# Two layers of a hybrid attention, Fourier and state-space block: the rotated queries as two products, and three moved pieces of work

## The chip, the cores and the metric

The kernel runs on one core of a Trainium2 chip. The metric is the device time of one execution in microseconds (us). The engines are TensorE (PE; PEld is its weight load), VectorE (DVE), ScalarE (ACT), GpSimd (POOL) and SyncE (SP), which issues DMAs.

## The reference, cut to what matters

Two layers; each has a mixer of three branches (attention with low-rank queries and keys, a Fourier mix, a state-space scan) and an MLP. The change is in the attention. Every head has a query of 64 plain and 32 rotary channels; the rotary key is shared by all eight heads.

```python
def apply_rope(x, cos, sin):
    h = QK_ROPE // 2
    x1, x2 = x[..., :h], x[..., h:]
    return jnp.concatenate([x1 * cos - x2 * sin, x2 * cos + x1 * sin], axis=-1)

def attend(q_nope, q_rope, k_nope, k_rope, v):
    s = jnp.einsum('bqhd,bkhd->bhqk', q_nope, k_nope)
    s = s + jnp.einsum('bqhr,bkr->bhqk', q_rope, k_rope)
    p = jax.nn.softmax(s * ATTN_SCALE, axis=-1)
    return jnp.einsum('bhqk,bkhd->bqhd', p, v)
```

There are 512 latent and 256 context tokens, 768 keys in all. Latent queries see all keys, context queries the 256 context keys. Layer 0 updates the context as well, so its attention has 768 queries; layer 1 has the 512 latent ones. The branches are projected, gated, summed and projected again.

## The kernel before

Activations lie with channels on partitions and tokens along the free dimension. Values that enter a large product are split into a high and a low part (`hh` and `hl`, `qqh` and `qql`, `kkh` and `kkl`), and each product is three: high by high, low by high, high by low. Weights come as tiles of 128x1024 through SyncE's queue (`raw`); GpSimd splits each into `whi` and `wlo`. All engines run hand-written programs, one instruction stream each, joined by semaphores; no scheduler moves anything.

The attention of a layer `l` goes through four head pairs `h2` (two heads each), and within a pair through units `u`, one for each block of 128 queries and head: 12 units in layer 0, 8 in layer 1. One unit is:

- TensorE: `scores` (L1062) into PSUM, two units ahead; the transposes of the normalised probabilities (L1162), into `TURNED_AT`; from unit 5 on `mix` (L1083), the product with the values, in thirds.
- VectorE: `maximum` (L2203): the row maximum `mx` and its negative; later the reciprocal of the sum (L2227) and the normalisation of `pr` (L2232).
- ScalarE: `exponent` (L1742), which writes `pr` and the row sum, and the copy of the transposed probabilities to `pt` (L1793).

In between, each pair prepares the next one. TensorE projects queries (`project_q`), keys (`project_k`) and values (`project_v`, L972) into spare PSUM; all of `project` records as L944. The projection gives a query's 96 rows and, on rows 96 to 127, the same rotary channels in swapped order. VectorE's `rotate` (L1947) makes the rotated query out of them, in place: rows 64 to 95 times the cosine table (L1949), rows 96 to 127 times the signed sine table into `qqt` (L1951), and the sum (L1954). ScalarE's `copy_query` then writes rows 0 to 95 to `qqh` (L1662), and VectorE's `low_query` the rest to `qql` (L2159). For the context queries of layer 0 `rotate_ends` and `low_ends` do the same. Keys go the same way: `copy_keys` (L1657) and `low_keys` (L2187), 64 rows for each head; rows 64 to 95 of the key tiles hold the shared rotated key, which is split once by VectorE (L2119 to L2125) and moved by four DMAs of ScalarE's queue into the other key tiles (`move_shared_keys`, L1679 to L1687) just ahead of the attention.

Where the next pair's preparation stands: in layer 0 keys at units 8 and 9, queries at 9 to 11 and after the last unit, context queries at 3 and 4 of their own pair. In layer 1 queries at units 2 to 5, keys and values at 6 and 7. The attention output of the pair before, on PSUM page 3, is split by `copy_mixed` (L1677) and `low_mixed` (L2193, `oal`). In the last pair ScalarE also makes the high parts of the other two branches' outputs (`osh`, `ofh`, L1785) and VectorE their low parts (`osl` L2266, `ofl` L2276), which the branch projections after the attention read. At the start of the attention VectorE's order is: low keys of both heads, rotation of both queries, low part of both queries.

## Time and profile before

| | us |
|---|---|
| median of three runs | 2210.8 |
| lowest and highest | 2208.2, 2213.7 |
| the profiled execution | 2214.1 |
| its span, first to last instruction | 2212.3 |
| TensorE busy in the span | 2140.5 |
| VectorE, ScalarE, GpSimd busy | 1262.1, 503.9, 901.2 |

The attention of layer 0 runs from about 420 to 600 us of the span, that of layer 1 from about 1600 to 1735. In a row of the timeline stand the start and the duration in us, the engine, the line, the operation, output and inputs, the count, and in brackets how long the engine was idle before and who released it. "issue" there means that the profile shows nothing that it waited for. TensorE's two clock levels are 1.2 and 2.4 GHz; PEclk is the granted share, 0.50 or 1.00.

### The profile page before, as it was taken

What the parts mean: (1) busy time and instruction counts of PE and PEld (TensorE: products, weight loads), DVE (VectorE), ACT (ScalarE), POOL (GpSimd) and SP (SyncE); (2) the same over time, 40 slices, a digit from 0 to 9 for tenths busy, and PEclk for the clock granted to TensorE, in tenths of its full rate; (3) what the DMA queues carried; (4) which work ended last, traced back from release to release, by engine and by line L of the source; (5) the groups of instructions that cost most, each with busy time, mean ns of one, the idle gap of its engine ahead of it and who ended that gap; (6) DMA issues with size and microseconds to landing.
All of it is one profiled execution on the core that took longest, in us unless ns stands there. A gap on an engine that the chain in (4) does not pass through costs nothing.

```text
span 2212.3 us, 30758 instructions
## 1 busy us (share of the span) xinstructions
PE 2140.5 (97%) x12532; PEld 1777.4 (80%) x12532; DVE 1262.1 (57%) x1935; ACT 503.9 (23%) x820; POOL 901.2 (41%) x492
## 2 busy tenths in 40 slices
PE   6999999999999999999999999999988999999998
PEld 4888888866688888888888888888766787888886
DVE  6998981466763546354565433793365756353453
ACT  4115122344400220110201112412354312010010
POOL 2441442200243354444444443454501356766662
PEclk9999999999999999999999999999999999999998
DMA  7363363233453432212233345445400552322221
GB/s 277 103 136 102 115 212 113 97 111 117 169 197 122 161 120 86 67 67 86 86 91 110 113 165 196 110 175 166 142 15 22 175 186 87 106 98 100 97 95 67
DMA packets 105775, 268.79 MB, mean 121 GB/s; under 512 B 22778, under 2 KB 42618, under 8 KB 103854
## 3 DMA queue, kind: packets, MB, share of 16 engines
q1 hardware_dynamic: 68928, 190.87, 25.3%
q10 hardware_dynamic: 36718, 76.06, 10.5%
q8 instruction: 99, 1.62, 0.3%
q14 instruction: 30, 0.25, 0.0%
HBM read 227.56 MB, written 37.88 MB: 120 GB/s over the span
## 4 chain that ended last, share of the span: by engine, by line
PE 85%; DVE 10%; ACT 1%; DMA 1%; issue 1%; SPq 0%; POOL 0%; ACTq 0%; DVEq 0%; POOLq 0%
PE ps L490 66%; PE ps L1080 3%; PE ps L944 2%; PE ps L1098 2%; PE ps L499 2%; PE ps L1162 2%; DVE t_in L2387 2%; DVE t_out L2387 2%; PE ps L608 2%; PE ps L803 1%; PE ps L985 1%; PE ps L505 1%; PE ps L1020 1%; PE ps L972 1%; PE ps L933 1%
## 5 line engine op out<-in xcount | busy, mean ns | idle before, releaser
L1355 POOL TENSOR_SCALAR whi<-raw 128x1024 fp32r<-128x1024 f32 x244 | 272.2, 1116 | 1258.5 <-PE ps L490 680.0
L1358 POOL TENSOR_TENSOR wlo<-raw,whi 128x1024 fp32r<-128x1024 f32 x244 | 629.5, 2580 | 20.4
L490 PE MATMUL ps<-hh,whi 128*128 128x512 f32 (+1 forms) x1560 | 464.3, 354 | 0.3 <-DVE ada L634 0.3
L490 PE MATMUL ps<-hl,whi 128*128 128x512 f32 (+1 forms) x1560 | 461.3, 352 | 0.0
L490 PE MATMUL ps<-hh,wlo 128*128 128x512 f32 (+1 forms) x1560 | 461.3, 352 | 0.0
L490 PEld LDWEIGHTS ps<-hh,whi 128*128 128x128 f32 x1560 | 253.7, 188 | 43.8 <-ACT mr L1843 1.0
L490 PEld LDWEIGHTS ps<-hh,wlo 128*128 128x128 f32 x1560 | 253.9, 188 | 42.6
L490 PEld LDWEIGHTS ps<-hl,whi 128*128 128x128 f32 x1560 | 253.9, 188 | 42.4 <-issue 0.2
L2320 DVE SCALAR_TENSOR_TENSOR x<-ps,ada,x 128x512 f32<-128x512 f32 x120 | 75.5, 659 | 344.3 <-PE ps L490 344.3
L490 PE MATMUL ps<-midh,whi 128*128 128x512 f32 (+1 forms) x768 | 232.3, 357 | 2.9 <-DVE midl L2350 2.9
L490 PE MATMUL ps<-midh,wlo 128*128 128x512 f32 (+1 forms) x768 | 231.1, 355 | 0.0
L490 PE MATMUL ps<-midl,whi 128*128 128x512 f32 (+1 forms) x768 | 230.8, 355 | 0.0
L2346 DVE TENSOR_TENSOR ms<-mr 128x768 f32<-128x768 f32 (+1 forms) x64 | 77.8, 1215 | 177.6 <-ACT mr L1843 177.5
L2350 DVE TENSOR_TENSOR midl<-ms,midh 128x768 fp32r<-128x768 f32 (+1 forms) x64 | 176.2, 2754 | 2.2
L1843 ACT ACTIVATE mr<-ps 128x768 f32<-128x768 f32 (+1 forms) x64 | 45.1, 705 | 519.4 <-PE ps L490 510.4
L490 PEld LDWEIGHTS ps<-midh,whi 128*128 128x128 f32 x768 | 125.9, 188 | 27.2 <-DVE midl L2350 4.6
L490 PEld LDWEIGHTS ps<-midh,wlo 128*128 128x128 f32 x768 | 126.2, 188 | 21.4
L490 PEld LDWEIGHTS ps<-midl,whi 128*128 128x128 f32 x768 | 126.0, 188 | 21.2
L1563 ACT ACTIVATE gt<-ps,b_gate 128x768 f32<-128x768 f32 (+1 forms) x48 | 38.2, 796 | 271.0 <-PE ps L490 259.3
L2208 DVE TENSOR_REDUCE mx<-ps 128x1 f32<-128x768 f32 (+1 forms) x80 | 67.9, 849 | 55.8 <-PE ps L1080 55.5
L1793 ACT COPY pt<-ps 128x768 f32<-128x768 f32 (+1 forms) x80 | 57.2, 716 | 113.7 <-PE ps L1162 113.4
L1379 ACT ACTIVATE sqt<-x 128x768 f32<-128x768 f32 (+1 forms) x40 | 30.1, 759 | 200.3 <-DVE x L2320 180.5
(263 smaller groups left out, 2993.1 us busy)
## 6 DMA issues: line engine op xcount, KB each, us to landing
raw<-in_w_main SPq DMA_DIRECT2D x244, 512.0 KB, 3.3
ada_gap<-in_ada_w SPq DMA_DIRECT2D x40, 512.0 KB, 9.8
ada_mixer<-in_ada_w SPq DMA_DIRECT2D x32, 512.0 KB, 4.0
g_d<-gt ACTq DMA_DIRECT2D x24, 384.0 KB, 2.4
gl<-g_d ACTq DMA_DIRECT2D x8, 1152.0 KB, 5.5
ada_first<-in_ada_w SPq DMA_DIRECT2D x16, 512.0 KB, 15.5
cout_d<-cz SPq DMA_DIRECT2D x12, 512.0 KB, 5.1
cout<-cout_d ACTq DMA_DIRECT2D x6, 1024.0 KB, 9.2
```

What stands on the lines that cost most here:

```text
L490: ins = pe.matmul(ps[:, p % 4, a:b], ww[:, w % W_SLOTS, kw * P:(kw + 1) * P], xx[:, kx, a:b], start=(first and i == 0 and j == 0), stop=(l ...
L499: pe.matmul(ps[:, p, a:b], ww[:, w % W_SLOTS, k * P:(k + 1) * P], hh[:, k, a:b], start=(k == 0 and ww is whi), stop=False)
L1080: ins = pe.matmul(flat[:, s0 + a:s0 + e], q, k[0:96, a:e], start=(i == 0), stop=(i == 2))
L1355: pool.tensor_scalar(whi[:, u, :], raw[:, u % 2, :], 1.0, 0.0, ALU.mult, ALU.add).then_inc(w_split.sem, 1)
L1358: pool.tensor_tensor(wlo[:, u, :], raw[:, u % 2, :], whi[:, u, :].bitcast(F32), ALU.subtract).then_inc(w_split.sem, 1)
L1793: act.copy(pts[pt_slot(l, h2, g)][:, j, k0:6, q0:q0 + P], flat[:, TURNED_AT + k0 * P:TURNED_AT + TOK].rearrange("p (k q) -> p k q", q=P)). ...
L1843: act.activation(mr[:, m % 2, 0:n], pair(t % mlp_pairs(l), n), ACT.Relu).then_inc(relu_ready.sem, relu_ready.mark((l, q, m)))
L2208: dve.tensor_reduce(mx[:, c:c + 1], flat[:, s0 + (0 if b < 4 else 512):s0 + TOK], AXX, ALU.max).then_inc(max_ready.sem, max_ready.mark((l, ...
L2320: ins = dve.scalar_tensor_tensor(x[:, m, a:b], pair(p, n)[:, a:b], ada[:, l, ada_tile(row, m), s:s + 1], x[:, m, a:b], ALU.mult, ALU.add)
L2346: dve.tensor_tensor(ms[:, m % 2, 0:n], mr[:, m % 2, 0:n], mr[:, m % 2, 0:n], ALU.mult).then_inc(msq_ready.sem, msq_ready.mark((l, q, m)))
L2350: dve.tensor_tensor(midl[:, m, 0:n], ms[:, m % 2, 0:n], midh[:, m, 0:n].bitcast(F32), ALU.subtract).then_inc(midl_ready.sem, midl_ready.ma ...
L2387: do(dve, dve.tensor_tensor(o, a, b, op), key or ("step", steps_done[0]))
```

## The change

Four things:

- The rotation keeps its two products. One VectorE multiplication over rows 64 to 127 replaces the three operations; `qqh` and `qql` take all 128 rows, and `scores` contracts 128 rows instead of 96. So that both products meet the same key, the shared key stands twice, on rows 64 to 95 and on 96 to 127: VectorE makes two casts more, one cast is wider, and the four DMAs move 64 rows instead of 32.
- In layer 1 the keys of the next pair are projected before the mix of unit 6 instead of behind it.
- In layer 1 `low_mixed` of the pair before moves from unit 2 to unit 3.
- In the last pair the other branches' copies and subtractions stand at the units of the tables `OTHERS_HIGH` and `OTHERS_LOW`, instead of 1 to 6 and 2 to 4.

```diff
+OTHERS_HIGH, OTHERS_LOW = ((5, 6, 7, 8, 9, 10), (0, 1, 5, 6, 6, 7)), ((6, 7, 8), (1, 5, 6))
...
-                qh, ql = (v[0:96, j, b * P:b * P + P] for v in (qqh[r], qql[r]))
+                qh, ql = (v[:, j, b * P:b * P + P] for v in (qqh[r], qql[r]))
...
-                        ins = pe.matmul(flat[:, s0 + a:s0 + e], q, k[0:96, a:e], start=(i == 0), stop=(i == 2))
+                        ins = pe.matmul(flat[:, s0 + a:s0 + e], q, k[:, a:e], start=(i == 0), stop=(i == 2))
...
+                    if l and h2 < 3 and u == 6:
+                        pe.wait_ge(exp_ready.sem, exp_ready.at((l, h2, 6)))
+                        project_k(h2 + 1, KEYS_AT)
                     if u >= 5 and (u - 5) % 4 < 3:
                         mix(h2, (u - 5) // 4, (u - 5) % 4)
...
                         if u == 6:
-                            pe.wait_ge(exp_ready.sem, exp_ready.at((l, h2, 6)))
-                            project_k(h2 + 1, KEYS_AT)
                             pe.wait_ge(q_lo.sem, q_lo.at((l, h2 + 1, "main1")))
                             project_v(h2 + 1, SPARE_AT[1], range(4), "first")
...
-                act.copy(qqh[h2 % 2][0:96, j, 0:m], flat[0:96, at:at + m]).then_inc(
+                act.copy(qqh[h2 % 2][:, j, 0:m], flat[:, at:at + m]).then_inc(
...
-                act.wait_ge(kr_split.sem, kr_split.at((l, 2)))
-                act.dma_start(kkh[0][64:96, :, :].bitcast(F32), kkh[1][64:96, :, :].bitcast(F32)).then_inc(kr_moved.sem, kr_moved.mark((l, 0), 16))
+                act.wait_ge(kr_split.sem, kr_split.at((l, 4)))
+                act.dma_start(kkh[0][64:128, :, :].bitcast(F32), kkh[1][64:128, :, :].bitcast(F32)).then_inc(kr_moved.sem, kr_moved.mark((l, 0), 16))
...
-                    if h2 == 3 and 1 <= u < 7:
-                        i = u - 1
+                    for i in [i for i in range(6) if h2 == 3 and OTHERS_HIGH[l][i] == u]:
...
-            dve.wait_ge(kr_split.sem, kr_split.at((l, 1)))
-            dve.tensor_copy(kkh[1][64:96, 1, :], kkh[1][64:96, 0, :].bitcast(F32)).then_inc(
+            dve.tensor_copy(kkh[1][96:128, 0, :], kkh[1][64:96, 0, :].bitcast(F32)).then_inc(
                 kr_split.sem, kr_split.mark((l, 2)))
+            dve.wait_ge(kr_split.sem, kr_split.at((l, 2)))
+            dve.tensor_copy(kkh[1][64:128, 1, :], kkh[1][64:128, 0, :].bitcast(F32)).then_inc(
+                kr_split.sem, kr_split.mark((l, 3)))
+            dve.tensor_copy(kkl[1][0][96:128, :], kkl[1][0][64:96, :].bitcast(F32)).then_inc(
+                kr_split.sem, kr_split.mark((l, 4)))
...
-                rotate(dve, flat[:, at:at + m], flat[:, at:at + m], qqt[h2 % 2][:, j], m, ("q", l, h2, f"main{j}"))
+                dve.tensor_tensor(flat[64:128, at:at + m], flat[64:128, at:at + m], rope[64:128, 0:m], ALU.mult).then_inc(
+                    ropes.sem, ropes.mark(("q", l, h2, f"main{j}")))
...
+                    if l and h2 and u == 3:
+                        low_mixed(h2 - 1)
...
-                    if l and h2 and u == 2:
-                        low_mixed(h2 - 1)
-                    if h2 == 3 and 2 <= u < 5:
-                        i = u - 2
+                    for i in [i for i in range(3) if h2 == 3 and OTHERS_LOW[l][i] == u]:
```

`rotate_ends` and `low_ends` change in the same way as `rotate_query` and `low_query`.

How the instructions stand in a row, before and after. First VectorE at the start of layer 0's attention (`kkl` low keys, `qqt` the second product, `qql` low queries, `mx` the row maximum); before:

```order
L2187 TENSOR_TENSOR kkl_98<-ps,kkh_96 64x768 [waits k_hi]
L1949 TENSOR_TENSOR ps<-ps,rope 32x768 [waits q_done]
L1951 TENSOR_TENSOR qqt_105<-ps,rope 32x768
L1954 TENSOR_TENSOR ps<-qqt_105,ps 32x768 [waits ropes]
L1949 TENSOR_TENSOR ps<-ps,rope 32x768 [waits w_used]
L1951 TENSOR_TENSOR qqt_105<-ps,rope 32x768
L1954 TENSOR_TENSOR ps<-qqt_105,ps 32x768 [waits ropes]
L2159 TENSOR_TENSOR qql_103<-ps,qqh_101 96x768 [waits q_hi] x2
L2208 TENSOR_REDUCE mx<-ps 128x1 [waits sc_done]
```

and after:

```order
L2178 TENSOR_TENSOR kkl_98<-ps,kkh_96 64x768 [waits k_hi]
L2156 TENSOR_TENSOR ps<-ps,rope 64x768 [waits q_done]
L2156 TENSOR_TENSOR ps<-ps,rope 64x768 [waits w_used]
L2161 TENSOR_TENSOR qql_103<-ps,qqh_101 128x768 [waits q_hi] x2
L2199 TENSOR_REDUCE mx<-ps 128x1 [waits sc_done]
```

Four of six operations between the low keys and the low queries are gone.

Second, VectorE in layer 1's second head pair, from the maximum of unit 4 (`oal` is the low part of the attention output of the pair before, `rsm` and `pr` the normalisation); before:

```order
L2211 TENSOR_SCALAR nmx<-mx 128x1 [waits max_ready]
L1949 TENSOR_TENSOR ps<-ps,rope 32x512 [waits q_done]
L1951 TENSOR_TENSOR qqt_105<-ps,rope 32x512
L1954 TENSOR_TENSOR ps<-qqt_105,ps 32x512 [waits ropes]
L2193 TENSOR_TENSOR oal<-ps,oah 128x512 [waits oh_ready]
L2227 RECIPROCAL rsm<-sm 128x1 [waits exp_ready]
L2232 TENSOR_SCALAR pr<-pr,rsm 128x768 [waits rsum_ready]
L2208 TENSOR_REDUCE mx<-ps 128x1 [waits sc_done]
L2211 TENSOR_SCALAR nmx<-mx 128x1 [waits max_ready]
L2159 TENSOR_TENSOR qql_103<-ps,qqh_101 96x512 [waits q_hi]
```

and after:

```order
L2202 TENSOR_SCALAR nmx<-mx 128x1 [waits max_ready]
L2156 TENSOR_TENSOR ps<-ps,rope 64x512 [waits q_done]
L2218 RECIPROCAL rsm<-sm 128x1 [waits exp_ready]
L2223 TENSOR_SCALAR pr<-pr,rsm 128x768 [waits rsum_ready]
L2199 TENSOR_REDUCE mx<-ps 128x1 [waits sc_done]
L2202 TENSOR_SCALAR nmx<-mx 128x1 [waits max_ready]
L2184 TENSOR_TENSOR oal<-ps,oah 128x512 [waits oh_ready]
L2161 TENSOR_TENSOR qql_103<-ps,qqh_101 128x512 [waits q_hi]
```

Ahead of the normalisation one operation stands instead of four; `oal` is now between the next maximum and the low query.

Third, TensorE at unit 6 of layer 1's first pair (`zkvh`, `zkvl` with `whi`, `wlo` are the keys' projection, `pt,vv` the mix, `vw` the values' weights); before:

```order
L1162 MATMUL ps<-early,pr 128x128 x5
L1098 MATMUL ps<-pt_111,vv_107 64x256 x4
L944 MATMUL ps<-zkvh,whi 128x512 [waits w_split,exp_ready]
...
L944 MATMUL ps<-zkvh,wlo 128x256
L972 MATMUL ps<-vw_113,zkv 128x128 [waits vw_in1,q_lo]
```

and after:

```order
L1160 MATMUL ps<-early,pr 128x128 x5
L941 MATMUL ps<-zkvh,whi 128x512 [waits w_split,exp_ready]
...
L941 MATMUL ps<-zkvh,wlo 128x256
L1095 MATMUL ps<-pt_109,vv_105 64x256 x4
L969 MATMUL ps<-vw_111,zkv 128x128 [waits vw_in1,q_lo]
```

The twelve key products and the mix have changed places.

## Rows read from the trace of the kernel before

**Rows 1.** page, part 1: each engine's busy time, share of the span, instructions

```profile
PE 2140.5 (97%) x12532; PEld 1777.4 (80%) x12532; DVE 1262.1 (57%) x1935; ACT 503.9 (23%) x820; POOL 901.2 (41%) x492
```

**Rows 2.** waits of TensorE, 420 to 600 us: total, times, longest

```profile
PE ps L1080 <- issue: 3.0, 3, 1.0
PE ps L1162 <- DVE pr L2232: 2.8, 4, 1.3
```

**Rows 3.** waits of TensorE, 1600 to 1735 us

```profile
PE ps L1162 <- DVE pr L2232: 8.4, 9, 2.0
PE ps L1080 <- DVE kkl L2187: 5.2, 3, 1.7
```

**Rows 4.** timeline, start of layer 0's attention

```profile
419.44 2.84 PE L972 MATMUL ps<-vw,zkv 128*128 128x128 f32 x24
422.83 0.97 DVE L1954 TENSOR_TENSOR ps<-qqt,ps 32x768 f32<-32x768 f32 x1
423.82 1.82 DVE L2159 TENSOR_TENSOR qql<-ps,qqh 96x768 fp32r<-96x768 f32 x2
424.93 0.62 PE L1080 MATMUL ps<-kkh,qqh 96*128 96x512 f32 x2 [2.64 <-DVE qql L2159]
```

**Rows 5.** by windows: length, busy of PE, PEld, DVE, ACT, POOL, then PEclk

```profile
424.90:435.50 10.60, 10.23 (x36) 8.73 (x37) 6.34 (x12) 5.38 (x9) 0.00 (x0) 0.52 0.05 14
```

**Rows 6.** timeline of TensorE, first and fifth scores of an attention

```profile
435.51 0.64 PE L1080 MATMUL ps<-kkh,qqh 96*128 96x512 f32 x2
1603.80 0.59 PE L1080 MATMUL ps<-kkh,qqh 96*128 96x512 f32 x2 [2.11 <-DVE qql L2159]
1611.27 0.59 PE L1080 MATMUL ps<-kkh,qqh 96*128 96x512 f32 x2
```

**Rows 7.** timeline, boundary between layer 0's first two head pairs

```profile
468.10 0.59 PE L1080 MATMUL ps<-kkh,qqh 96*128 96x512 f32 x2 [0.99 <-issue]
469.43 0.96 DVE L2208 TENSOR_REDUCE mx<-ps 128x1 f32<-128x768 f32 x1 [0.38 <-PE ps L1080]
471.49 0.96 DVE L2208 TENSOR_REDUCE mx<-ps 128x1 f32<-128x768 f32 x1 [0.19 <-PE ps L1080]
473.79 1.38 PE L972 MATMUL ps<-vw,zkv 128*128 128x128 f32 x10 [0.50 <-DVE oal L2193]
```

**Rows 8.** timeline, GpSimd and VectorE in layer 0's second pair

```profile
483.96 2.37 POOL L1358 TENSOR_TENSOR wlo<-raw,whi 128x1024 fp32r<-128x1024 f32 x1
485.07 1.69 DVE L2232 TENSOR_SCALAR pr<-pr,rsm 128x768 f32<-128x768 f32 x1
```

**Rows 9.** timeline, rotation in layer 1's second pair

```profile
1652.45 0.60 PE L1080 MATMUL ps<-kkh,qqh 96*128 96x512 f32 x2
1654.27 0.69 DVE L2193 TENSOR_TENSOR oal<-ps,oah 128x512 fp32r<-128x512 f32 x1
1656.66 0.68 DVE L2159 TENSOR_TENSOR qql<-ps,qqh 96x512 fp32r<-96x512 f32 x1
1657.51 0.40 PE L944 MATMUL ps<-zqh,whi 128*128 128x512 f32 x1
```

**Rows 10.** timeline, end of layer 1's second pair

```profile
1671.07 1.94 DVE L2187 TENSOR_TENSOR kkl<-ps,kkh 64x768 fp32r<-64x768 f32 x2 [4.74 <-ACT kkh L1657]
1673.06 0.62 PE L1080 MATMUL ps<-kkh,qqh 96*128 96x512 f32 x2 [1.73 <-DVE kkl L2187]
```

**Rows 11.** waits of TensorE 1706 to 1735 us, and timeline of its end

```profile
PE ps L1162 <- DVE pr L2232: 1.7, 2, 1.2
...
1732.30 0.62 ACT L1785 CAST ofh<-of 128x512 fp32r<-128x512 f32 x1
1733.76 0.84 PE L1162 MATMUL ps<-early,pr 128*128 128x128 f32 x6 [0.24 <-ACT pt L1793]
```

**Rows 12.** kkl's DMA issues (tile view), and the page's part 6

```profile
DMA to landing us min/median/max: 2.5/2.6/4.2
...
ada_first<-in_ada_w SPq DMA_DIRECT2D x16, 512.0 KB, 15.5
```

More of the change, by code:

```diff
@@ L239, in build @@
         qql = [at(f"qql{r}", HREG + (18432, 30720)[r], [P, 2, TOK], F32R) for r in range(2)]
-        qqt = [at(f"qqt{r}", HREG + (18432, 30720)[r], [P, 2, TOK]) for r in range(2)]
         vv = (at("vv0", HREG + 24576, [P, TOK // P, P]), rest("vv1", 55296, [P, TOK // P, P]))
@@ L473, in build @@
         flat = ps[:].rearrange("p a b -> p (a b)")
-        def banks(at, a, b):
-            cut = (at + a) // 512 * 512 + 512 - at
-            return [(a, b)] if cut >= b else [(a, cut)] + banks(at, cut, b)
         def spans(n):
@@ L1660, in copy_query @@
             def copy_query(h2, j, at, m):
-                act.wait_ge(ropes.sem, ropes.at(("q", l, h2, f"main{j}", 2)))
-                act.copy(qqh[h2 % 2][0:96, j, 0:m], flat[0:96, at:at + m]).then_inc(
+                act.wait_ge(ropes.sem, ropes.at(("q", l, h2, f"main{j}")))
+                act.copy(qqh[h2 % 2][:, j, 0:m], flat[:, at:at + m]).then_inc(
                     q_hi.sem, q_hi.mark((l, h2, f"main{j}")))
             def copy_ends(h2, at):
-                act.wait_ge(ropes.sem, ropes.at(("q", l, h2, "ends", 2)))
-                act.copy(qqh[h2 % 2][0:96, :, LAT:TOK], flat[0:96, at:at + 512].rearrange("p (j t) -> p j t", j=2)).then_inc(
+                act.wait_ge(ropes.sem, ropes.at(("q", l, h2, "ends")))
+                act.copy(qqh[h2 % 2][:, :, LAT:TOK], flat[:, at:at + 512].rearrange("p (j t) -> p j t", j=2)).then_inc(
                     q_hi.sem, q_hi.mark((l, h2, "ends")))
@@ L2163, in rotate_ends @@
                 dve.wait_ge(w_used.sem, w_used.at(l * N_TILES + pair_tile(h2)))
-                src = flat[:, at:at + 512].rearrange("p (j t) -> p j t", j=2)
-                second = qqt[h2 % 2][:, :, LAT:TOK]
-                key = ("q", l, h2, "ends")
-                def table(p0):
-                    return rope[p0:p0 + 32, LAT:TOK].unsqueeze(1).to_broadcast([32, 2, CTX])
-                dve.tensor_tensor(second[64:96], src[96:128], table(96), ALU.mult).then_inc(
-                    ropes.sem, ropes.mark((*key, 0)))
-                dve.tensor_tensor(src[64:96], src[64:96], table(64), ALU.mult).then_inc(
-                    ropes.sem, ropes.mark((*key, 1)))
-                dve.wait_ge(ropes.sem, ropes.at((*key, 1)))
-                dve.tensor_tensor(src[64:96], second[64:96], src[64:96], ALU.add).then_inc(
-                    ropes.sem, ropes.mark((*key, 2)))
+                src = flat[64:128, at:at + 512].rearrange("p (j t) -> p j t", j=2)
+                dve.tensor_tensor(src, src, rope[64:128, LAT:TOK].unsqueeze(1).to_broadcast([64, 2, CTX]),
+                                  ALU.mult).then_inc(ropes.sem, ropes.mark(("q", l, h2, "ends")))
             def low_ends(h2, at):
                 dve.wait_ge(q_hi.sem, q_hi.at((l, h2, "ends")))
-                dve.tensor_tensor(qql[h2 % 2][0:96, :, LAT:TOK], flat[0:96, at:at + 512].rearrange("p (j t) -> p j t", j=2),
-                                  qqh[h2 % 2][0:96, :, LAT:TOK].bitcast(F32), ALU.subtract).then_inc(
+                dve.tensor_tensor(qql[h2 % 2][:, :, LAT:TOK], flat[:, at:at + 512].rearrange("p (j t) -> p j t", j=2),
+                                  qqh[h2 % 2][:, :, LAT:TOK].bitcast(F32), ALU.subtract).then_inc(
                                       q_lo.sem, q_lo.mark((l, h2, "ends")))
```

6 lines of the change are left out of this document (3 added, 3 removed).

## The prediction, made before the changed kernel had run

> **What bounds the kernel now.** I read the page's first part, then TensorE's waits in the two attention stages, then the timeline around each wait, then the clock. TensorE is busy for 97% of the span [rows 1], so only what shortens its work or fills its idle time counts. The change touches two stretches, the attention of layer 0 (about 420 to 600 us) and of layer 1 (1600 to 1735 us). In the first, TensorE waits for the low part of the query (2.64 us) [rows 4], three times ahead of the second scores of a head pair (3.0), four times for the normalised probabilities `pr` (2.8) [rows 2], and three times for `oal` (one of 0.50 stands in [rows 7]). In the second it waits nine times for `pr` (8.4), three times for the keys' low part (5.2) [rows 3] and once for the query (2.11) [rows 6]. Behind most of them stands one VectorE queue in which the rotation is three operations in a row. A second loss is no wait: from 424.9 to 435.5 us the granted clock is 0.52, so TensorE works at its lower level, 1.2 GHz [rows 5], right after the idle 2.64 us [rows 4].
>
> All terms below are in the time of the profiled execution, 2214.1 us (span 2212.3). It lies 3.3 us above the median of the three runs, 2210.8, and I take those 3.3 us off at the end.
>
> **Term A, start of layer 0's attention: 2.6 us.** Each rotation is three operations of 0.97 us [rows 4]; one is left. It has 64 partitions instead of 32; a subtraction over 64 partitions of the same length takes 0.97 too [rows 10], so I cost width in partitions at nothing. The first pair's rotations lie on the path: the second can start when its projection ends (TensorE turns to the values at 419.44), takes 0.97, and the first low part (0.95) follows at about 420.6 and ends at 421.5. The values keep TensorE until about 422.3 [rows 4]. So the wait of 2.64 goes and the values are the bound. Next late is the second low part (about 422.4, one product of 1.1 us after it is needed at the earliest), still covered.
>
> **Term B, layer 0's clock: 3.1 us.** From the first scores to the fifth, layer 0 needs 10.58 us (424.93 to 435.51), layer 1 with the same instructions 7.47 (1603.80 to 1611.27) at full clock, although it too idles 2.11 us ahead of them [rows 6]. After the change layer 0 has less idle time there than layer 1 has now, so I take the upper level: 10.58 - 7.47 = 3.1. The lower bound is zero. The Trainium skill ("TensorE: Matmul & The Clock Gate", Part 1) says that low activity brings the lower level and that the monitor runs freely, not from the kernel's start. By that rule equal idle time may fall on either side, which is why this is a term of its own and why the first rival exists. The rows above are one case of each.
>
> **Term C, three boundaries between head pairs in layer 0: 3.6 us.** After the last query projection VectorE rotates, ScalarE copies, VectorE subtracts, and the second scores start 0.99 us late [rows 7]. Two operations of 0.70 us less more than cover that. Then VectorE's queue hangs on these scores: their maximum 1.33 us after their start, the normalisation, the next maximum after an idle 0.19 us, `oal`, and behind it TensorE's value projection at 473.79 [rows 7]. The second scores start 0.99 earlier, the idle 0.19 closes, 1.2 us each time. The three waits there (a third, for an exponent, is 0.7) are 2.2 us; I don't count the rest, because the chain moves as a whole.
>
> **Term D, the context queries of layer 0: 2.8 us.** `rotate_ends` stands ahead of the normalisation of unit 4. The four waits of 2.8 us in all [rows 2] each lie within the 1.4 us that two removed operations give (the largest is 1.3), and in the last pair the copies and subtractions of the other branches move to later units as well, where TensorE has queued work. One of the four is not only the rotation's: the normalisation at 485.07 took 1.69 us, GpSimd's `wlo` ran until 486.33, and it ended behind it [rows 8]. The normalisation now comes 1.4 us sooner, between GpSimd's two operations, and I take it as free of them. The Trainium skill ("SBUF — State Buffer", Who interferes with whom) makes this an exclusive lock between VectorE and GpSimd, which goes to whoever asks first. The trace agrees. By the same rule the lock could be lost again at the new place. The bound from the rows is then 1.26 less: D between 1.5 and 2.8.
>
> **Term E, start of layer 1's attention: 2.1 us.** The same as A: the wait is 2.11 us [rows 6], the two rotations lose 1.4 us each, and the first low part is ready before the values end.
>
> **Term F, head pairs of layer 1: 4.6 us.** Of the 8.4 us of waits for `pr`, 1.7 are in the last pair [rows 11], so 6.7 in the first three. The unit after a rotation waits up to 2.0 us [rows 3]. Removing 1.46 us of rotation, and 0.69 us of `oal` that now stands one unit later [rows 9], removes the wait, but something else is next: the following query projection needs the low part of the first query. That comes after the maximum of the next scores (1.33 us after their start as in [rows 7], some 1.0 long), `oal` (0.69) and its own 0.68 us. In the second pair: scores at 1652.45, so the low part ends at about 1656.4, and the projection starts there instead of at 1657.51 [rows 9]. That gives 1.1 us; without `oal`, in the first pair, I take 1.2, because a copy of ScalarE then ends last. The second rotation's wait of 0.4 goes in each (the rest of the 6.7 us). 1.6 + 1.5 + 1.5 = 4.6; bounds 3 and 6.5.
>
> **Term G, last head pair of layer 1: 0.6 us.** `oal` and two of the subtractions leave the busy units, and 1.7 us of waits shrink [rows 11]. But ScalarE now has two casts of 0.62 us instead of one ahead of the last but one copy of transposed probabilities, for which TensorE already waits 0.24 us [rows 11]. Of about 1.2 us, 0.6 are given back. Bounds 0 and 1.7.
>
> **Edits costed at nothing.** The keys ahead of the mix (three times): both are TensorE work with nothing idle between, 1.0 us of mix and 2.2 us of keys change places. On ScalarE the copies of the keys still stand behind the copy of the next transposes, VectorE's low parts behind them (1671.07), and TensorE still waits 1.73 us for these (1673.06) [rows 10]. The exponent for which the keys wait is ready before. If that cover were gone, up to 1.0 us each. The shared key rows: four casts instead of two on VectorE, each under 1 us by their length; TensorE has no wait at all from there to the attention, so they lie under its gate projections. The scores contract 128 rows instead of 96: projections with 128 rows run at the same pace per column.
>
> **The doubled move of key rows.** Four transfers of 192, 96, 96 and 96 KB become twice as large. No row shows 64 partitions of this. The nearest landing times are 2.5 to 4.2 us [rows 12]; the last is issued at about 414.4, so it lands by 418.6, against the 422.3 us at which the scores now want it. The cover is 3.7 us, and in layer 1 a little over 2 us. Zero if the larger ones land like these; if time doubles, to 8.4 us, the scores start 0.5 us late in layer 0 and 1.9 in layer 1. I take zero, nearest to the median. The Trainium skill ("SBUF — State Buffer", Door 1) says that partitions 64 to 127 reach no more ports than 64 to 95. By that page the move takes twice as long, which is the second rival. No run so far shows it.
>
> **Sum.** 2.6 + 3.1 + 3.6 + 2.8 + 2.1 + 4.6 + 0.6 = 19.4 us. 2214.1 - 19.4 = 2194.7 profiled; 2191.4 as a median. The stages after attention are TensorE-bound, so the gain stays.
>
> **Rivals.**
> 1. *The clock does not come back, or falls elsewhere.* TensorE still idles 1.7 us at the end of three head pairs in layer 1, and other short falls shift with the phase. For: one pair of idle times decided each way. Against: less idle than in a stretch that kept its clock. Without B: 16.3, so 2194.5; with one more such fall 2197.5. 0.2.
> 2. *The key rows land late.* Costs 0.5 + 1.9 us and, since TensorE then idles again, half the time term B: 19.4 - 2.4 = 17.0, or 13.9 with B, so 2194 to 2197. 0.15.
> 3. *The next chain holds more than I counted.* ScalarE's exponents, copies of queries and of transposed probabilities are interleaved in a fixed order. If half of C, D and F (11.0) stays, 13.9 remain: 2196.9. For: F already shows such a takeover. Against: ScalarE is the least busy of the engines on the page, 23% [rows 1]. 0.12.
> 4. *Slower.* The moves land as late as the worst kind of transfer on the page, 15.5 us [rows 12], behind the weight transfers that fill the queues at 415 to 422 us. The scores then start at 429.9 instead of 424.9, and at 1610.7 instead of 1603.8: 11.9 us lost, C, D, F and G give back 11.6, and layer 1's start falls to the lower clock as layer 0's did, 3.1 more: 3.4 us slower, 2214.2. It decides from a landing of about 15 us; nothing under 4.2 comes near. 0.02.
> 5. *The move of keys and copies is all that does something and the rotation was covered.* The waits' releasers, `qql` and `pr` behind the rotation, speak against it; it would leave 2 us or less: 2209. 0.02.
>
> **How the numbers follow.** The forecast, 2191.4, has 0.49. The range for 8 in 10: upward past rivals 1 to 3, to 2199; downward, if all waits named above vanish (C 6.5, F 6.5, G 1.7) some 6 us more, and if layer 1's short falls of the clock go too, a few more, 2185. A measurement of this kernel can tell a change from none from about 0.3%, 6.6 us. Below 2204.2: forecast, rivals 1 to 3 nearly whole, 0.95. Within 0.3%: 0.04. Slower by more: 0.01.
>
> **What would show it.** In the trace after: no wait for `qql` ahead of the first scores of either layer; clock 1.0 from about 422 us on, and the fifth scores some 7.5 us after the first; 0.99 gone at the boundaries; waits for `pr` in layer 0 under 0.5 us in all, in layer 1 under 2; the 1.73 us for `kkl` unchanged; a new short wait for `qql` ahead of the second query projection in layer 1. A landing of the key rows after 422 us, or a first-scores wait released by a DMA, would make A, B and E wrong together.

## The result, and the profile after

| | before | changed kernel |
|---|---|---|
| median, six runs each | 2212.58 us | 2199.31 us |
| lowest to highest | 2208.22 to 2214.79 | 2195.13 to 2205.19 |
| profiled execution (its span) | 2214.1 (2212.3) | 2202.57 (2200.8) |

The ratio is 0.9944, 95% interval 0.9926 to 0.9962: faster, by 12.4 us. The forecast was 19.4 us less, 2191.4, with a range of 2185 to 2199. The direction held; the gain was 7 us short, and the time stands just above the range.

The same text of the kernel was run again beside the first experiments (run e1 below), and gave 0.9924, 0.9907 to 0.994, a gain of 16.8 us (the two medians alone lie 19.8 us apart). The intervals overlap, so the change is worth some 12 to 17 us by these two ratios.

Page of the changed kernel, part 1 (busy us, share of the span, instructions). VectorE has 34 instructions and 32 us less than in [rows 1]:

```profile
PE 2144.0 (97%) x12532; PEld 1780.9 (81%) x12532; DVE 1230.3 (56%) x1901; ACT 503.7 (23%) x820; POOL 902.5 (41%) x492
```

Waits of TensorE in the changed kernel, first 420 to 600 us, which answers to [rows 2], then 1585 to 1735 us, which answers to [rows 3] (releaser: total us, times, longest):

```profile
PE ps L1077 <- DMA kkl<-kkl: 2.3, 1, 2.3
PE ps L1077 <- ACT pr L1746: 1.7, 4, 0.7
PE ps L1160 <- DVE pr L2223: 1.4, 4, 0.5
...
PE ps L1095 <- DVE qql L2172: 1.0, 3, 0.3
...
PE ps L1077 <- DVE kkl L2178: 5.2, 3, 1.7
PE ps L969 <- issue: 2.7, 1, 2.7
...
PE ps L941 <- DVE qql L2161: 0.8, 2, 0.4
PE ps L1160 <- ACT pt L1790: 0.8, 1, 0.8
PE ps L1160 <- DVE pr L2223: 0.7, 2, 0.5
```

Much is as forecast: the 0.99 us at layer 0's boundaries (`issue`, 3.0) are gone, the waits for `pr` fell from 8.4 to 0.7 in layer 1, `kkl` kept its 5.2, and the new short wait for `qql` ahead of layer 1's second query projection is there (0.8). In layer 0 the waits for `pr` fell only from 2.8 to 1.4, where under 0.5 was forecast. Two lines were not in the sum: the first scores of layer 0 wait 2.3 us for a **DMA of the key rows**, and TensorE idles 2.7 us ahead of the first values of layer 1, against 1.3 before.

Timeline of the changed kernel at the start of layer 0's attention: ScalarE's queue (ACTq issues DMAs), then SyncE's, then TensorE (here and in the other timelines rows are picked out):

```profile
414.92 0.56 ACTq L1680 DMA_DIRECT2D kkh<-kkh  x1
415.51 2.25 ACTq L1682 DMA_DIRECT2D kkl<-kkl  x2
417.79 1.03 ACTq L1684 DMA_DIRECT2D kkl<-kkl  x1
418.86 1.62 ACT L1655 CAST kkh<-ps 64x768 fp32r<-64x768 f32 x2 [4.42 <-issue]
...
417.78 2.71 SPq L1288 DMA_DIRECT2D ada_mixer<-in_ada_w  x3
...
421.67 2.84 PE L969 MATMUL ps<-vw,zkv 128*128 128x128 f32 x24
426.83 1.01 PE L1077 MATMUL ps<-kkh,qqh 128*128 128x512 f32 x2 [2.33 <-DMA kkl<-kkl]
```

In the kernel before the same four issues stand so (timeline, ScalarE's queue):

```profile
412.54 0.58 ACTq L1682 DMA_DIRECT2D kkh<-kkh  x1
413.15 1.25 ACTq L1684 DMA_DIRECT2D kkl<-kkl  x2
414.43 0.62 ACTq L1686 DMA_DIRECT2D kkl<-kkl  x1
415.09 1.62 ACT L1657 CAST kkh<-ps 64x768 fp32r<-64x768 f32 x2 [3.03 <-issue]
```

The larger moves take longer to *issue*: 3.84 us for the four instead of 2.45, so the casts of the first pair's keys stand behind 4.42 us instead of 3.03. Here the first two take what they took before; only the third and the last take longer (up to 1.60 and 1.03 us instead of some 0.6 each). And the last one is issued in the same instant as the first of three 512 KB weight loads on SyncE's queue. It is in only just ahead of the scores at 426.83, 9 us later. Tile view of `kkl` in the changed kernel, issues of the second and third move in both layers (ns, shortest, median, longest) and the landing of all `kkl` moves (us):

```profile
L1682 ACTq DMA_DIRECT2D kkl<-kkl x4: 615/1006/1600, 415.5 to 1590.9; - x4
...
DMA to landing us min/median/max: 4.5/5.9/9.0
```

The DMA issues of the two kernels in this stretch (KB each, median us to landing), after and before:

```profile
ada_mixer<-in_ada_w SPq DMA_DIRECT2D x3, 512.0 KB, 9.0
kkl<-kkl ACTq DMA_DIRECT2D x3, 192.0 KB, 6.9
```

```profile
ada_mixer<-in_ada_w SPq DMA_DIRECT2D x3, 512.0 KB, 6.4
kkl<-kkl ACTq DMA_DIRECT2D x3, 96.0 KB, 2.6
```

How much of the 9 us is the doubled rows and how much the meeting with the weight loads was not tried apart. In layer 1, where a single 512 KB load stands beside them and not four, the three `kkl` moves landed after 4.8, 6.3 and 5.4 us, against 2.5 to 4.2 before. So some 5 to 6 us come with the doubled rows, and the meeting is my reading of the rest.

In layer 1 the first delay alone decides. Timeline of the changed kernel, ScalarE and TensorE:

```profile
1593.36 1.61 ACT L1655 CAST kkh<-ps 64x768 fp32r<-64x768 f32 x2 [5.20 <-issue]
...
1596.30 4.44 PE L969 MATMUL ps<-vw,zkv 128*128 128x128 f32 x24 [2.67 <-issue]
1600.38 0.81 PE L1077 MATMUL ps<-kkh,qqh 128*128 128x512 f32 x2
```

The values of layer 1 wait for the low part of the keys, this for the casts, and these for the issues (1.3 us of this idle stood in the kernel before as well). The 24 products of the values then take 4.44 us where layer 0's take 2.84: the clock is at its lower level.

**Where the time went, by stretches.** All kernels here give TensorE 12,532 matmuls. So the same matmul can be found in each trace by its number, and the stretches compared. *Start* is from the first product of the values (in layer 1 from five matmuls ahead of it, so that its wait is inside) to the fifth scores in layer 0 and to the first scores in layer 1; *rest* is from there to the end of that attention. In brackets: the number of stretches of about 3.4 us at half clock (1.2 GHz) that fell into it. "Outside" is all else of the span.

| profiled execution | start L0 | rest L0 | start L1 | rest L1 | outside | span |
|---|---|---|---|---|---|---|
| before | 16.06 (3) | 164.69 | 7.61 | 131.34 (3) | 1892.6 | 2212.3 |
| changed | 13.64 (1) | 158.79 | 8.05 (1) | 125.54 (3) | 1894.7 | 2200.8 |
| e1 changed, again | 11.55 | 158.70 | 5.58 | 121.48 | 1895.2 | 2192.6 |
| e2 rows copied by VectorE | 10.06 | 158.47 | 5.35 | 121.52 | 1895.8 | 2191.2 |
| e3 larger moves alone | 16.81 (3) | 166.00 (2) | 9.22 (1) | 130.00 (2) | 1894.9 | 2216.9 |
| e4 rotation alone | 13.72 (1) | 158.65 | 8.26 (1) | 123.32 (1) | 1901.0 | 2205.1 |
| e5 = e2, keys read early | 10.06 | 158.53 | 5.36 | 115.42 | 1894.3 | 2183.7 |
| e6 moves behind casts | 13.70 (1) | 158.75 | 6.03 | 124.11 (2) | 1892.3 | 2195.0 |
| e7 before, VectorE copies | 16.19 (3) | 164.80 | 7.85 | 129.64 (2) | 1892.6 | 2211.1 |
| e8 = e5, keys behind mix | 10.08 | 158.47 | 5.36 | 115.58 | 1893.2 | 2182.8 |
| e9 changed, keys read early | 12.04 | 158.65 | 7.77 (1) | 115.81 | 1889.5 | 2183.8 |
| e10 before, keys read early | 14.97 (2) | 164.66 | 7.05 | 124.27 (2) | 1894.0 | 2204.9 |
| e11 = e8, no order moves | 10.05 | 158.27 | 5.35 | 115.60 | 1896.2 | 2185.5 |

The table holds the whole case. Columns 1 to 4 repeat within about half a microsecond wherever edit, key rows' landing and clock agree, which no median does; "outside", where the change adds only casts of the key rows on VectorE, scatters over 12 us.

### The profile page after: what moved, and what is told of

It reads as the page before. It is cut to its first block, busy times and chain, and to the rows that moved or that the text cites. A ratio compares the mean times of both kernels' runs of the same rounds, so it can differ in the third digit from the quotient of the medians.

```text
span 2200.8 us, 30724 instructions
## 1 busy us (share of the span) xinstructions
PE 2144.0 (97%) x12532; PEld 1780.9 (81%) x12532; DVE 1230.3 (56%) x1901; ACT 503.7 (23%) x820; POOL 902.5 (41%) x492
## 4 chain that ended last, share of the span: by engine, by line
PE 88%; DVE 7%; DMA 2%; ACT 1%; issue 1%; SPq 0%; POOL 0%; ACTq 0%; DVEq 0%; POOLq 0%
PE ps L487 66%; PE ps L1077 3%; PE ps L941 2%; PE ps L1095 2%; PE ps L496 2%; PE ps L605 2%; PE ps L1160 2%; DVE t_out L2377 1%; DVE t_in L2377 1%; PE ps L969 1%; PE ps L502 1%; PE ps L982 1%; PE ps L800 1%; PE ps L1017 1%; DMA raw<-in_w_main 1%; DVE mx L2199 1%
```

## The experiments

Theory after the result: the doubled move of the key rows, costed at nothing, eats terms A and E and part of B, by its issue time and by its late landing; the rest of the gap is the clock in layer 1, set off by the unchanged waits for `kkl`. Rivals: the rotation itself is worth less than summed; the order moves (keys ahead of the mix, copies in other units) cost something.

The runs e1 to e4, e5 to e8 and e9 to e11 are three groups, each with its own runs of the kernel before beside it. Ratios are to those; medians are compared within a group only. Ratios of which the intervals overlap do not part two kernels; there the stretches decide.

### e1 to e4: taking the change apart

**e1** is the changed kernel again.

> The changed kernel once more, as the yardstick of this chip. Theory 1 (the doubled move of key rows took terms A and E and a third of B): the gain stays at 10 to 14 us, the trace again shows a wait of 2 us or more ahead of layer 0's first scores, released by a DMA, and a wait of about 2.7 us ahead of layer 1's value projection. Theory 2 (the missing 7 us were chance, elsewhere in the span): the gain moves toward 19 us.

Measured: 2194.43 us (six runs, 2192.0 to 2199.8) beside 2214.22 for the kernel before. The gain, 16.8 us, lies between what the two theories gave, 10 to 14 and 19. The key rows are late here too, but the first scores wait 1.2 us for their DMA, not 2.3, the idle ahead of layer 1's values is 1.6 us, not 2.7, both less than theory 1 had, and the clock stays up.

The rest of layer 1 takes 121.48 us instead of 125.54 with the same three waits of 1.73 us: in the one trace each of them was followed by 3.4 us at half clock, in the other none.

**e2** copies the key rows with VectorE, which stood idle for 18 us there.

```diff
-                act.dma_start(kkh[0][64:128, :, :].bitcast(F32), kkh[1][64:128, :, :].bitcast(F32)).then_inc(...)
-                ... three more for kkl
+            dve.tensor_copy(kkh[0][64:128, :, :], kkh[1][64:128, :, :].bitcast(F32))
+            for j in range(2):
+                dve.tensor_copy(kkl[0][j][64:128, :], kkl[1][0][64:128, :].bitcast(F32))
+            dve.tensor_copy(kkl[1][1][64:128, :], kkl[1][0][64:128, :].bitcast(F32)).then_inc(
+                kr_moved.sem, kr_moved.mark((l, 2)))
```

> The changed kernel, but the shared key rows are copied to the other key tiles by VectorE (four copies, after the last gate tile, in its idle time) instead of by four DMAs of ScalarE's queue. Theory 1: ScalarE's copies of the keys start when the key projection ends, about 2 us earlier in layer 0 and 3 us earlier in layer 1 than with the doubled DMAs; the first scores follow the values without a wait in both layers; 5 to 8 us faster than the changed kernel, 17 to 21 us faster than before. Theory 2: within 2 us of the changed kernel.

Measured: 2191.63 us, ratio 0.9903 (0.9885 to 0.992), 2.8 us less than e1 where I had expected 5 to 8; the intervals of the two overlap, and the four stretches say 1.9 (297.3 and 295.4). The trace shows what I was after: no wait ahead of the first scores, clock 1.00, and the two starts at 10.06 and 5.35 us. VectorE and TensorE in e2's timeline, and the window from the first to the fifth scores (length, busy of PE, PEld, DVE, ACT, POOL, then PEclk), which answers to [rows 5]:

```profile
412.99 0.96 DVE L2140 CAST kkh<-kkh 64x1536 fp32r<-64x1536 f32 x1 [18.09 <-issue]
413.86 4.09 DVE L2142 CAST kkl<-kkl 64x768 fp32r<-64x768 f32 x2
417.87 0.55 DVE L2143 CAST kkl<-kkl 64x768 fp32r<-64x768 f32 x1
418.45 1.94 DVE L2175 TENSOR_TENSOR kkl<-ps,kkh 64x768 fp32r<-64x768 f32 x2
...
421.05 2.84 PE L969 MATMUL ps<-vw,zkv 128*128 128x128 f32 x24
423.65 0.59 PE L1077 MATMUL ps<-kkh,qqh 128*128 128x512 f32 x2
...
423.70:431.10 7.40, 5.91 (x38) 4.85 (x37) 5.82 (x12) 5.76 (x9) 1.23 (x1) 1.00 0.15 57
```

Against the first profile of the changed kernel the four stretches say 10.6 us (306.0 and 295.4). I expected too much because e1 lost less at the starts (1.7 us against e2) than the first profile of the same kernel (6.3: 3.6 and 2.7). The cost of the doubled move is that spread.

**e3** puts only the doubled key rows and moves into the kernel before.

> The kernel before with the doubled key rows and their doubled DMAs alone; rotation, scores and all order as before (the scores still read 96 rows). Theory 1: VectorE's low keys and rotations start 1 to 2 us later in both layers, 2 to 5 us slower than before. Theory 2: no change, within 1 us.

Measured: 2215.19 us, ratio 1.0007 (0.999 to 1.0024). In the trace the wait for `qql` at layer 0's start grew from 2.6 to 4.1 us and the start of layer 1 by 1.6, since the rotation chain begins behind ScalarE's later casts. The ratio puts it at 1.5 us, below the 2 to 5 that theory 1 gave, and its interval holds both no change and 5 us: the median decides nothing here, only the trace shows the delay.

**e4** keeps the rotation and undoes the three order moves (keys behind the mix; copies and subtractions of the other branches back in units 1 to 6 and 2 to 4; `oal` back in unit 2).

> The changed kernel without its three moves of order (keys behind the mix again, oal at unit 2, other branches' copies at their old units). If the moves of order are worth what I gave them: 1 to 2 us slower than the changed kernel, since only the last pair of layer 1 and the last of layer 0 gain by them, and 11 to 13 us faster than before. If they carry the gain instead of the rotation: 6 us or more slower than the changed kernel.

Measured: 2195.36 us, ratio 0.9925 (0.9911 to 0.9939), the same as e1, 16.6 us faster than before; I had expected 11 to 13, and 1 to 2 slower than the changed kernel. Layer 1's rest is 123.32 us with one half-clock stretch, against 121.48 with none. Its waits for `pr` are longer (3.0 against 0.8 us), but some of that comes back in the waits that e1 has and e4 has not (`qql` 0.8, `pt` 0.8 against 0.2). The whole gain is the rotation's, within the 3 us or so that the two intervals leave open.

The traces show why. The last pair of layer 1 (from about 20 us ahead of the end) is 0.57 us shorter than before with the order moves (changed kernel, e1, e2) and 0.04 without them (e4, e11). The second and third pair each gain 1.7 us with `oal` at unit 3 and 1.9 with it at unit 2: behind the wait for `pr` that goes, a wait of 0.38 us for `qql` comes. The two nearly cancel.

### e5 to e8: the reader of the keys, and the move

In the changed kernel the keys of layer 1's next pair are projected ahead of the mix, and nobody reads them sooner. Timeline of e2, end of layer 1's first pair:

```profile
1615.10 1.08 PE L1095 MATMUL ps<-pt,vv 128*64 128x256 f32 x8
1618.86 0.80 ACT L1779 COPY pt<-ps 128x768 f32<-128x768 f32 x1 [4.04 <-PE ps L1160]
1619.56 1.61 ACT L1655 CAST kkh<-ps 64x768 fp32r<-64x768 f32 x2
1620.38 1.94 DVE L2175 TENSOR_TENSOR kkl<-ps,kkh 64x768 fp32r<-64x768 f32 x2 [4.71 <-ACT kkh L1655]
1622.38 0.62 PE L1077 MATMUL ps<-kkh,qqh 128*128 128x512 f32 x2 [1.73 <-DVE kkl L2175]
```

The keys are done when the mix begins, at 1615.1; ScalarE waits 4.04 us for the next transposes and only then casts them. **e5** is e2 with this edit:

```diff
-                    if l and h2 < 3 and u == 7:
-                        copy_keys(h2 + 1, 1, KEYS_AT)
+                    if l and h2 < 3 and u == 6:
+                        copy_keys(h2 + 1, 0, KEYS_AT)
+                        copy_keys(h2 + 1, 1, KEYS_AT)
...
-                        if u == 6:
-                            copy_keys(h2 + 1, 0, KEYS_AT)
```

> The kernel of e2 with one edit: in layer 1 ScalarE casts both heads' keys of the next pair in unit 6 ahead of that unit's copy of pt, where until now the first cast stood behind the copy of unit 6 and the second in unit 7 (one from the front of the tail). The keys have been projected ahead of the mix since the change, so in e2 they stood ready from 1615.0, while ScalarE stood idle 4.04 us at the pt copy (1618.86) and cast them at 1619.56. Theory (the early projection was worth nothing only because its reader came late in ScalarE's order): the three waits of 1.73 us of the scores for kkl go (5.2 us together), and the half-clock stretches that followed them in the profile of after (three of 3.4 us) can't come: 5 us less than e2, 2186 to 2187, if the casts are done by 1617 and VectorE's kkl by 1619. Rival 1 (the next thing is late too: with the kkl gone the chain maximum, exponent, pr of the new pair's first unit is what the tail waits for): 1 to 2 us less, 2190. Rival 2 (VectorE's two kkl come between pr of unit 7 and the maxima and delay nothing, but the copy of the values or of pt of unit 6 is pushed back): no change.

Measured: 2185.35 us, ratio 0.988 (0.9863 to 0.9896): 5 us less than e2 by the ratios (their intervals overlap), 6.0 by the four stretches (289.4 and 295.4). The same place in e5:

```profile
1613.86 1.61 ACT L1655 CAST kkh<-ps 64x768 fp32r<-64x768 f32 x2 [0.39 <-PE ps L941]
1614.69 1.94 DVE L2174 TENSOR_TENSOR kkl<-ps,kkh 64x768 fp32r<-64x768 f32 x2 [0.37 <-ACT kkh L1655]
1617.52 0.80 ACT L1780 COPY pt<-ps 128x768 f32<-128x768 f32 x1 [2.04 <-PE ps L1160]
1619.06 0.59 PE L1077 MATMUL ps<-kkh,qqh 128*128 128x512 f32 x2
```

No wait ahead of the scores, 6.1 us off layer 1's rest (3 x 2.0), and no half clock there.

**e6** is the changed kernel with the four moves issued behind the two casts.

> The changed kernel with the four moves of the key rows still on ScalarE's queue, but issued behind the two casts of the first pair's keys and not ahead of them. Theory (the doubled rows cost through their landing, 9 us for the last one, not through ScalarE's time): the casts come 4.4 us earlier and the queries with them, but the last move is issued 1.6 us later and lands later, so the wait of the first scores grows from 1.2 to 2.3 up to 2.8 to 4 us and the half clock comes back: 2198 to 2202, slower than the after of e1 (2194.4). Rival (the cost is ScalarE's issue time, 3.8 us before the casts, and the landing is long only because the queue of layer 1 is full): 2191 to 2193, as e2. In layer 1, where the idle ahead of the values is put down to issue (1.6 to 2.7 us), the theory says nothing changes there or it grows; the rival says it goes back to 1.3.

Measured: 2199.28 us, ratio 0.9941 (0.9927 to 0.9954). The median is where the theory had it. In layer 0 the first scores wait 2.3 us for the DMA and the half clock comes back, though 2.8 to 4 us were expected; in layer 1 it separates the two costs. TensorE at layer 1's start in e6:

```profile
1591.44 2.84 PE L969 MATMUL ps<-vw,zkv 128*128 128x128 f32 x24
1596.34 0.62 PE L1077 MATMUL ps<-kkh,qqh 128*128 128x512 f32 x2 [2.06 <-DMA kkl<-kkl]
```

The idle ahead of the values is gone (it *was* the issue time ahead of the casts: here the rival was right), and the transfer's landing takes its place with 2.06 us. Either order loses; the doubled move costs issue time and landing time.

**e7** gives VectorE's copies to the kernel before.

> The kernel before with one edit: its key rows (32 of them) are copied by VectorE and not by four transfers on ScalarE's queue, as in e2. It prices the move without the rotation. Theory (in the kernel before the move is hidden behind the rotation chain, landing 2.6 us, and the first scores wait for qql): VectorE's three copies take 1.5 to 5 us ahead of the keys' kkl and would push its chain back unless they fit in the 23 us in which VectorE stood idle: within 2 us of before, 2212 to 2216 here. The rotation kept as rows is then worth 20 to 24 us of e2 minus this one. Rival (part of e2's gain is the move itself, by ScalarE's queue being free): 2206 to 2210, and the rotation is worth only 14 to 18.

Measured: 2216.27 us, ratio 1.0017 (1.0008 to 1.0026), 3.7 us slower, just past the upper end of what I expected. The wait for `qql` at layer 0's start is 3.3 instead of 2.6 us, and its stretches are within 0.3 us of the kernel before at both starts; the four together are 1.2 us shorter (318.5 and 319.7), so the profiled execution does not show where the 3.7 us are. So VectorE's copies are no gain by themselves. Between e7 and e2, the same copies without and with the change, lie 25 us by the two ratios and 23.1 us by the four stretches (318.5 and 295.4): that is the change without its doubled move. It includes the half clock: e7 has five such stretches there, e2 none.

**e8** is e5 with the keys projected behind the mix again.

> The kernel of e5 with the keys' projection of layer 1 put back behind the mix, ScalarE's casts still ahead of the pt copy of unit 6. Theory (the two moves are worth something only together): PE finishes the keys about 1.1 us later, at 1616.1, ScalarE casts them to 1617.8 and VectorE's kkl are done at 1619.6, still ahead of the scores at 1620.65: then most of the 5 us come from the reader alone and this equals e5 within 1 us. Rival (each microsecond of the projection counts, since ScalarE's pt copy of unit 6 and the values' copy queue behind the casts): 1.1 us for each of three tails, 3 us slower than e5.

Measured: 2184.57 us, ratio 0.9875 (0.9855 to 0.9896). Layer 1's rest is 115.58 us, e5's 115.42. The reader's place is worth 6 us, the projection's nothing, with the reader early or late.

### e9 to e11: the early read on the other kernels

**e9**: the changed kernel with e5's edit alone. **e10**: the kernel before with it. **e11**: e8 with the copies of the other branches and `oal` put back, so that no order move of the change is left.

> The changed kernel with only the two casts of layer 1's next keys ahead of unit 6's pt copy on ScalarE; its key rows are still moved by the four transfers. Theory (two separate losses that add: the late reader of the keys, three waits of 1.73 us and the half clock that they can set off, and the landing of the doubled key rows at both starts): the three waits of the scores for kkl are gone, 5.2 to 6 us, and with them the half-clock stretches of layer 1's attention, so 2187 to 2190 where the changed kernel gave 2194.4 beside e1; the wait for the DMA of kkl in layer 0 (1.2 to 2.3 us) stays. Rival (the losses share their cover, the key rows' lateness in layer 1 shifts the tails): 2 us or less, 2192 to 2194.

Measured: 2190.08 us, ratio 0.9896 (0.9875 to 0.9918). Layer 1's rest is 115.81, the starts (12.04 and 7.77) keep their loss. The two losses add, as the theory said; the median stands at the upper edge of what it gave.

> The kernel before with the same edit alone: its keys are projected behind the mix and its rotation has the three steps. Theory (the wait for kkl at the three tails is ScalarE's order alone, with or without the rotation): 5 us less than before, 2206 to 2209. Rival (before's tail is set by pr and by the rotation chain, 8.4 us of waits of the transposes for pr in layer 1; the 1.73 us go over into the wait for pr of the new pair): 0 to 2 us, 2211 to 2213.

Measured: 2207.51 us, ratio 0.9978 (0.9963 to 0.9993), 4.9 us less. Waits of TensorE in e10, layer 1:

```profile
PE ps L1162 <- DVE pr L2231: 8.4, 9, 2.0
PE ps L1080 <- DVE qql L2158: 2.1, 1, 2.1
```

The three waits for `kkl` are gone without being replaced, and the 8.4 us for `pr` stand as in [rows 3]: two separate losses.

> The kernel of e8 (VectorE's copies of the key rows, ScalarE's early casts, keys projected behind the mix) with the last two order moves undone too: the other branches' casts and subtractions back in units 1 to 6 and 2 to 4, and the mixed low part back in unit 2. Theory (the three order moves of the change are worth nothing that the median shows, as e4 against e1 has it): within 1.5 us of e8, 2183 to 2186.5. Rival (they are worth the 2.3 us by which the waits of the transposes for pr in layer 1 were longer in e4, 3.0 against 0.7 us): 2187.

Measured: 2187.22 us, ratio 0.9877 (0.9855 to 0.9899). The median is where the rival put it, the ratio is e8's, and the four stretches sum to 289.3 us against 289.5 for e8. The waits for `pr` in layer 1 are 3.0 us here and 0.7 there, and yet the attention is no longer. I follow the stretches: the order moves together are worth nothing that shows.

The best kernels are e5 and e8, 1.2% under the kernel before; their intervals lie wholly below those of the changed kernel.

## Why the prediction was right, and where it failed

The profiled executions compare directly: forecast 19.4 us, seen 11.5.

| part | forecast | changed | e1 | e2 |
|---|---|---|---|---|
| A + B, start of layer 0 | 5.7 | 2.4 | 4.5 | 6.0 |
| C + D, rest of layer 0 | 6.4 | 5.9 | 6.0 | 6.2 |
| E, start of layer 1 | 2.1 | -0.4 | 2.0 | 2.3 |
| F + G, rest of layer 1 | 5.2 | 5.8 | 9.9 | 9.8 |
| outside | 0 | -2.2 | -2.7 | -3.2 |
| sum | 19.4 | 11.5 | 19.7 | 21.1 |

That e1 comes to 19.7 is luck: A + B, the key rows' loss, is 1.2 short and "outside" took 2.7, while F + G hold 4.6 us of half clock that the kernel before had there and e1 has not, and that no term counted.

**The failed step is the doubled move of the key rows, costed at zero.** It took the landing time from [rows 12] and the *issue* at the old moment, "at about 414.4". But four transfers of twice the rows take 3.84 us of ScalarE's queue instead of 2.45. They stand ahead of the casts of the keys, on which the rotations of layer 0 and the values of layer 1 wait. And the last one, issued with the weight loads, lands after 9 us. So the bound from both sides held neither quantity: 9 us to landing in place of 2.6 to 4.2, and "zero" for the issue. The two starts are short by 3.3 (A + B) and 2.5 us (E), 5.8 of the 7.9 us that the profiled gain fell short; 2.2 more are "outside". Rival 2 was this case, with 0.5 + 1.9 us and half of B; the trace shows 2.33 us of waiting for the DMA in layer 0; in layer 1 no scores wait for it, and the loss is the idle ahead of the values, 2.67 us instead of 1.29, with the half clock behind it. The page that I cited for it ("SBUF — State Buffer", Door 1, of the Trainium skill) was right in direction: doubled moves landed in 6.9 instead of 2.6 us in layer 0 and in 5.4 instead of 2.6 in layer 1 (medians). It deserved more than 0.15, since a row for 64 partitions was missing and the cited rule spoke against the change.

**Term A** (2.6) was right in mechanism: the rotation chain no longer bounds the start, and in e2, without the DMA in its place, all of it is there. **Term B** (3.1) was right in size: e1 and e2 need 7.49 and 7.46 us from the first to the fifth scores, forecast 7.47. In the changed kernel's first trace 8.48, since the clock fell for 3.4 us after the wait for the DMA. **C and D** came as summed, within 0.5 us, and apart too: between the same matmuls the three boundaries are 3.66 us shorter (forecast 3.6) and the other parts 2.24 (forecast 2.8, bounds 1.5 to 2.8). In D a new wait of 0.3 us three times (the mix for `qql` of the context queries) was not foreseen, and 1.4 us of waits for `pr` stay. **E** failed with the key rows, by 2.5 us; e2 shows its 2.3.

**F and G** were right in size (5.2 forecast, 5.8 in the changed kernel, with three half-clock stretches before and after). Between the same matmuls F is 1.28 + 1.71 + 1.70 = 4.7 us (forecast 4.6) and G 0.57 (forecast 0.6). What I treated as noise is a term of its own: without half clock the stretch takes 121.5, another 4.1 us less, or 1.35 us for each fall. The falls follow the unchanged waits of 1.73 us in one execution and not in the next. Rival 1 had this, "one more such fall 2197.5", at the price of layer 0's three stretches together, and it came together with rival 2. I had given them separate chances, though at both starts the half clock stands right behind the delay of rival 2.

**Keys ahead of the mix**: nothing, as costed (e8). The other order moves were not costed at nothing: G's 0.6 is theirs and came, but `oal` in the later unit gave back 0.2 us in each of two pairs, so that e4 and e11 show nothing of them. **Outside** the attention the first profile of before was among the short ones (1892.6; the others 1889.5 to 1901.0), which takes 2 us off every profiled comparison and was not foreseeable from one trace.

What stays open: how much of the difference between the 12.4 us of the first measurement and the 16.8 of e1 is chance. The traces say that the same kernel can lose 8.7 us more in the attention in one execution than in another (306.0 and 297.3 us), through landing and clock alone.

## What to carry to other kernels

When a change makes a transfer larger, cost three things: its time on the queue that issues it (and who stands behind it there), the new moment of the issue, and which transfers it then meets. An operation that is moved ahead gains nothing while its reader on the next engine comes late; here the reader's move alone (e8) brought the whole 6 us. Look for the long idle of that engine right in front of the reader. And compare traces by stretches between the same matmuls: that settled here, to half a microsecond, what medians with intervals of 0.3% could not.

## What the runs showed of the hardware that I had not expected

**Short idle times and the clock.** Idle of TensorE ahead of the first scores, and the half clock that followed, over the runs: none (e2, e5, e8, e11): none. 1.2 and 1.7 us (e1, e9): none. 2.3, 2.3 and 2.4 (changed, e6, e4): 3.4 us each. 2.6 and 3.3 and 4.1 (before, e7, e3): 10.2 us; 2.8 (e10): 6.8. But 2.06 and 2.11 in layer 1 (e6, before): none, and 1.73 anything: three falls of three in the changed kernel, two in e6 and in the kernel before, one in e4 and in e3, none in e1, e2 and e7. Ahead of layer 1's values: up to 1.6 us (before, e1, e2, e5 to e8, e10, e11), none; 2.6 to 3.0 (changed, e3, e4, e9), 3.4 us each. So no length of idle parts the cases between 1.7 and 2.1 us from those that fell. One window of the changed kernel behind such a wait:

```profile
1631.50:1635.00 3.50, 3.50 (x14) 2.19 (x14) 1.11 (x2) 0.99 (x2) 0.00 (x0) 0.51 0.11 37
```

**VectorE's copies beside GpSimd.** In e2 two copies of 64x768 took 4.09 us together and the third, of the same size, 0.55. GpSimd worked until 417.52 in that time (timeline of e2, GpSimd):

```profile
413.08 1.77 POOL L1353 TENSOR_SCALAR whi<-raw 128x1024 fp32r<-128x1024 f32 x1 [4.77 <-issue]
414.94 2.58 POOL L1356 TENSOR_TENSOR wlo<-raw,whi 128x1024 fp32r<-128x1024 f32 x1
```

The Trainium skill's lock between the two ("SBUF — State Buffer", Who interferes with whom) agrees: the first copy ends with the first operation of GpSimd or soon after, the second behind its second. GpSimd pays too: that first operation took 1.77 us, and 1.04 us at 1588.90, with no copy beside it. The long pair of copies recurs in layer 1 (4.07 and 0.55) and in e7 (4.06 and 0.55), and it may be why e7 is slower than the kernel before; that was not tried.

**Two paces of the same matmuls.** Far from the attention, at full clock and with no waits, three pairs of products take 1.04 us in some stretches and 1.06 in others. Timelines of TensorE around 1240 us, two pairs of products with 29 others between them, in the kernel before (10.40 us apart) and in the changed one (10.60):

```profile
1238.21 0.51 PE L490 MATMUL ps<-hh,whi 128*128 128x512 f32 x2
...
1248.61 0.51 PE L490 MATMUL ps<-hh,whi 128*128 128x512 f32 x2
```

```profile
1238.06 0.51 PE L487 MATMUL ps<-hh,whi 128*128 128x512 f32 x2
...
1248.66 0.51 PE L487 MATMUL ps<-midh,whi 128*128 128x512 f32 x2
```

A pace lasts for tens to hundreds of microseconds, and many of its changes stand beside a wait or a half-clock stretch. The same matmuls between 1137 and 1330 us of the kernel before took 193.05 us there and 193.04 in e2, but 196.38 in e3. All three have one half-clock stretch in them and no wait, so the 3.3 us are the pace. The changed kernel took 194.76 with no half clock at all, and the other traces lie at 194.7 without it or at 196.3 to 196.4 with it; these 1.6 us are what the half clock costs in a stretch without waits. Differences of 3 us between single traces can be the pace alone. What sets the pace was not tried.
